# End of a chunked scan reordered: where the yT rows are converted, and where the projection begins

## The reference, cut to what matters

```python
# branch A, per chunk of 128 tokens (8 chunks for the prompt)
lmat   = exp(where(tril, diff, -inf))                       # decay masks, 16 heads
cb     = einsum('bclgn,bcsgn->bclsg', cm, bm)
y_diag = einsum('bclsg,bclsge,bcsgep->bclgep', cb, lmat, xdt)
final, prev = lax.scan(step, init_state, (chunk_decay, st)) # s = s * dec + add
y_off  = einsum('bclgn,bcgepn,bclge->bclgep', cm, prev, exp(acs))
y      = rmsnorm((y_diag + y_off + d_skip * xs) * silu(z), ssd_norm_w)
# merge
merged = g0 * (y_ssd @ w_br_ssd) + g1 * (y_att @ w_br_att) + g2 * (y_mem @ w_br_mem)
y      = rmsnorm(x + merged @ w_out, norm_f_w)
```

## Time and profile before

| | us |
|---|---|
| runs (3) | 2124.83, 2127.19, 2128.45; median 2127.19 |
| profiled execution | 2122.49, span 2120.6 |
| TensorE busy | 1978.7 (93% of the span) |
| VectorE, ScalarE, GpSimd busy | 984.6, 763.9, 241.5 |

### The profile page before, as it was taken

How to read it: one execution, slowest core, us unless ns; L and a number is a source line. 1 busy time by engine, 2 the same in 40 slices (tenths; PEclk the granted TensorE clock), 3 DMA queues, 4 the chain that set the end, 5 groups by cost and what they waited for, 6 DMA issues and landing times.

```text
span 2120.6 us, 34809 instructions
## 1 busy us (share of the span) xinstructions
PE 1978.7 (93%) x14301; PEld 1887.0 (89%) x14301; DVE 984.6 (46%) x1941; ACT 763.9 (36%) x1642; POOL 241.5 (11%) x358
## 2 busy tenths in 40 slices
PE   5999999999979999999999899999999859969997
PEld 5899999999979999999999898769999759969997
DVE  5313676535465353534236676103454545454423
ACT  5223354223343333323555322215566532132202
POOL 1001111100001010111111200001121111100000
PEclk9999999999999999999999999999999869989999
DMA  6211332311101111122246675683455536454422
GB/s 216 90 42 52 93 92 82 93 46 48 40 30 51 54 49 57 61 64 83 68 147 220 224 255 163 228 281 124 150 160 176 202 102 191 166 181 137 144 83 105
DMA packets 171742, 257.18 MB, mean 121 GB/s; under 512 B 20229, under 2 KB 115269, under 8 KB 171557
## 3 DMA queue, kind: packets, MB, share of 16 engines
q1 hardware_dynamic: 149328, 187.97, 28.1%
q0 software_dynamic: 22256, 66.98, 9.3%
HBM read 188.13 MB, written 66.76 MB: 120 GB/s over the span
## 4 chain that ended last, share of the span: by engine, by line
PE 76%; DVE 8%; ACT 6%; DMA 5%; issue 3%; SPq 0%; DVEq 0%; POOL 0%; ACTq 0%; POOLq 0%
PE bank L2287 19%; PE bank L2288 19%; PE bank L2289 19%; PE bank L2483 2%; DVE w_lo L1753 2%; PE bank L2698 2%; PE bank L2458 2%; DMA acc<-acc_T 2%; PE bank L2441 1%; PE bank L2587 1%; PE bank L2419 1%; ACT soft L1579 1%; PE bank L2742 1%; PE bank L2520 1%; DMA sums<-sum_T 1%
## 5 line engine op out<-in xcount | busy, mean ns | idle before, releaser
L2287 PE MATMUL bank<-w_hi,hT_hi 128*128 128x256 f32 (+1 forms) x1848 | 535.7, 290 | 1.4 <-issue 1.4
L2288 PE MATMUL bank<-w_lo,hT_hi 128*128 128x256 f32 (+1 forms) x1848 | 523.8, 283 | 0.0
L2289 PE MATMUL bank<-w_hi,hT_lo 128*128 128x256 f32 (+1 forms) x1848 | 522.9, 283 | 0.0
L2287 PE MATMUL bank<-hT_hi,w_hi 128*128 128x352 f32 x1344 | 450.8, 335 | 6.3 <-DVE acc L2134 5.6
L2289 PE MATMUL bank<-hT_hi,w_lo 128*128 128x352 f32 x1344 | 438.9, 327 | 0.0
L2288 PE MATMUL bank<-hT_lo,w_hi 128*128 128x352 f32 x1344 | 438.2, 326 | 0.0
L2287 PEld LDWEIGHTS bank<-w_hi,hT_hi 128*128 128x128 f32 (+1 forms) x1848 | 348.7, 189 | 3.2 <-issue 1.6
L2289 PEld LDWEIGHTS bank<-w_hi,hT_lo 128*128 128x128 f32 (+1 forms) x1848 | 349.6, 189 | 0.6
L2288 PEld LDWEIGHTS bank<-w_lo,hT_hi 128*128 128x128 f32 (+1 forms) x1848 | 348.7, 189 | 1.3
L2287 PEld LDWEIGHTS bank<-hT_hi,w_hi 128*128 128x128 f32 x1344 | 257.7, 192 | 20.1 <-issue 8.4
L2288 PEld LDWEIGHTS bank<-hT_lo,w_hi 128*128 128x128 f32 x1344 | 258.5, 192 | 0.5
(11 more groups left out here) (423 smaller groups left out, 2926.1 us busy)
## 6 DMA issues: line engine op xcount, KB each, us to landing
w_raw<-in_w_in SPq DMA_DIRECT2D x96, 512.0 KB, 5.0
kvring<-in_cache_win_kv SPq DMA_DIRECT2D x98, 256.0 KB, 4.7
feat_T<-fstage POOLq DMA_DIRECT2D x40, 528.0 KB, 4.0
fstage<-feat_T SPq DMA_DIRECT2D x16, 528.0 KB, 4.6
xc<-feat_T SPq DMA_DIRECT2D x8, 1024.0 KB, 5.8
sums<-sum_T SPq DMA_DIRECT2D x32, 256.0 KB, 4.5
o_rows<-obuf POOLq DMA_DIRECT2D x48, 132.0 KB, 2.0
mo<-o_rows SPq DMA_DIRECT2D x24, 264.0 KB, 3.6
```

The lines of the kernel that those rows point to most:

```text
L2287: pe.matmul(out, xh(k), wh(k), start=(k == 0), stop=False)
L2288: pe.matmul(out, xh(k), wl(k), start=False, stop=False)
L2289: ins = pe.matmul(out, xl(k), wh(k), start=False, stop=(k == nk - 1))
```

## The change

Up to the gates' last projection the list is the same. Behind it (ssd 6,1), (6,2), (5,6) and (6,3) come first, and the yT rows are loaded and converted behind them; four rows must be done for the first projection step, all eight for the fourth (before: eight for the first). The first three projection steps stand between, each alone. The two decay halves of chunk 7 are apart, the second between rows 5 and 6. The w_lo of the last gate chunk's successor comes behind (ssd 7,3). The slots of the rows follow `YA_SLOT`. The splits of chunks 52 to 55 are attached to their last step, and the remaining 45 steps are spread over 54 groups (before 52 steps and splits over 51 groups), with empty groups behind (7,5), (8,5), (8,6).

```diff
--- before.py
+++ after.py
@@ -113,6 +113,7 @@
 
 N_MEM_FILL, N_TAIL_FILL = 8, 2
 FILL_MERGE, FILL_KEYS, FILL_SOFT, FILL_VALUES = 3.75, 2.25, 1.25, 1.75
+YA_SLOT = (0, 1, 2, 0, 1, 0, 1, 0)
 PASSES = ((1, 4),)
 PASS_AT = {1: 0}
 
@@ -301,21 +302,13 @@
     for c in range(NB):
         core.append([("ssd", c, 0)] + ([("ssd", c - 1, 5)] if c else []))
         core += [[("ssd", c, 1 + i)] + [("decay", 0, i)] * (c == 0) for i in range(2)]
-        core.append(([("ssd", c - 1, 6)] if c else []) + [("ssd", c, 3)] + [("decay", c + 1, i) for i in range(2) if c + 1 < NB])
+        core.append(([("ssd", c - 1, 6)] if c else []) + [("ssd", c, 3)])
+        core[-1] += [("decay", c + 1, i) for i in range(2) if c + 1 < NB - 1]
         core.append([("ssd", c, 4)])
-    core += [[("ssd", NB - 1, 5)], [("ssd", NB - 1, 6)], [("ssd_state",)], [("ssd", NB, 0)]]
-    core += [[("ssd", NB, q)] for q in (1, 2, 3)]
-    core += [[(q, b)] for b in range(BS) for q in ("ssd_sb", "ssd_sd", "ssd_so")]
-    core += [[("ssd_st",)], [("ssd_sy",)]]
-    core += [[("ssd", NB, q)] for q in (4, 5, 6)] + [[], []] + [[("yb", k)] for k in range(KT8)]
-    n_gate, n_ya = 31, 4
+    n_gate = 5 * (NB - 2) + 1
     core[n_gate - 3] += [("yal", k) for k in range(3)]
-    for i in range(n_ya):
-        core[n_gate + i] += [("yal", k) for k in ((3, 4), (5, 6), (7,), ())[i]]
-        core[n_gate + i] += [("ya", 2 * i), ("ya", 2 * i + 1)]
     sched += spread(core[:n_gate], gate_steps(len(fill_src)))
-    for x in core[n_gate:n_gate + n_ya]:
-        sched += x
+    last_gate = len(chunks) - 1
     steps = []
     for i in range(4):
         n = chunk("p1", 2 * i, "att+mem", CW * i)
@@ -326,8 +319,19 @@
                     steps.append([("p1", n, f, br, j)])
                     if j == 0 and (ft, br) != (0, 0) and ft + br < KT8:
                         steps[-1].append(("p1g", ft + br, 1 - br))
-        steps.append([("split", n)])
-    sched += spread(core[n_gate + n_ya:], steps)
+        steps[-1].append(("split", n))
+    c = NB - 2
+    sched += [("ssd", c, 1), ("ssd", c, 2), ("ssd", c - 1, 6), ("ssd", c, 3)]
+    sched += [("yal", 3), ("ya", 0), ("yal", 4), ("ya", 1), ("ya", 2), ("yal", 5), ("ya", 3)] + steps[0]
+    sched += [("ssd", c, 4)] + steps[1] + [("decay", c + 1, 0), ("yal", 6), ("ssd", c + 1, 0), ("ssd", c, 5)] + steps[2]
+    sched += [("yal", 7), ("ya", 4), ("ya", 5), ("decay", c + 1, 1), ("ya", 6), ("ya", 7)]
+    core = [[("ssd", c + 1, 1)], [("ssd", c + 1, 2)], [("ssd", c, 6), ("ssd", c + 1, 3)], [("low", last_gate)], [("ssd", c + 1, 4)]]
+    core += [[("ssd", NB - 1, 5)], [], [("ssd", NB - 1, 6)], [("ssd_state",)], [("ssd", NB, 0)]]
+    core += [[("ssd", NB, q)] for q in (1, 2, 3)]
+    core += [[(q, b)] for b in range(BS) for q in ("ssd_sb", "ssd_sd", "ssd_so")]
+    core += [[("ssd_st",)], [("ssd_sy",)], [("ssd", NB, 4)], [("ssd", NB, 5)], [], [], [("ssd", NB, 6)], [], []]
+    core += [[("yb", k)] for k in range(KT8)]
+    sched += spread(core, steps[3:])
     for i in range(4):
         n = chunk("p2", 2 * i, "w_br_ssd", CW * i)
         sched += [("p2", n, f, j) for f in range(2) for j in range(3)] + [("split", n)]
@@ -966,7 +970,11 @@
             return (Lflat[:, D:2 * D] if b % 2 == 0 else yo[:, :]).rearrange("p (i n) -> p i n", i=8)
 
         def ya_slot(k):
-            return (yraw, acc1, acc0)[k % 3][:, :]
+            return (yraw, acc1, acc0)[YA_SLOT[k]][:, :]
+
+        def ya_loads(at, k):
+
+            return 16 * sum(YA_SLOT[x] == at for x in range(k))
 
         def acc_of(ft):
             return (acc0, acc1)[ft % 2]
@@ -1158,8 +1166,8 @@
                     if k == 0:
                         late_free(sp)
                     if k >= 3:
-                        sp.wait_ge(s_yal, k - 2)
-                    sp.dma_start(ya_slot(k), yT[8 + k]).then_inc(s_kv[k % 3], 16)
+                        sp.wait_ge(s_yal, 1 + max(x for x in range(k) if YA_SLOT[x] == YA_SLOT[k]))
+                    sp.dma_start(ya_slot(k), yT[8 + k]).then_inc(s_kv[YA_SLOT[k]], 16)
                     if k == 3:
                         gates_stored(sp)
                         load_gate(0, 0)
@@ -1655,12 +1663,12 @@
                     k = s[1]
                     if k == 0:
                         act.wait_ge(s_pj, n_act_proj)
-                    act.wait_ge(s_kv[k % 3], kv_loads(k % 3) + 16 * (k // 3 + 1))
+                    act.wait_ge(s_kv[YA_SLOT[k]], kv_loads(YA_SLOT[k]) + ya_loads(YA_SLOT[k], k + 1))
                     act.activation(yAh[:, k, :], ya_slot(k), ACT.Copy).then_inc(s_yah, 1)
                 elif s[0] == "yb":
                     k = s[1]
                     at = k % 3
-                    act.wait_ge(s_kv[at], kv_loads(at) + 16 * len(range(at, KT8, 3)) + 16 * (k // 3 + 1))
+                    act.wait_ge(s_kv[at], kv_loads(at) + ya_loads(at, KT8) + 16 * (k // 3 + 1))
                     if k == 6:
                         act.wait_ge(s_p1st[0], 16 * KT8 // 2)
                     act.activation(yBh[:, k, :], yb_slot(k), ACT.Copy).then_inc(s_yah, 1)
@@ -2130,7 +2138,7 @@
                         if ft >= 2 and j == 0:
                             dve.wait_ge(s_p1st[ft % 2], 16 * (ft // 2))
                         elif j == 0:
-                            dve.wait_ge(s_yal, KT8)
+                            dve.wait_ge(s_yal, 1 + max(x for x in range(KT8) if YA_SLOT[x] == 2 - ft))
                         dve.tensor_tensor(acc1[:, cols], psum, gate1[:, 0, cols], ALU.mult).then_inc(s_pjv, 1)
                     else:
                         dve.tensor_tensor(gate1[:, 1, cols], psum, gate1[:, 1, cols], ALU.mult).then_inc(s_pjv, 1)
@@ -2617,6 +2625,8 @@
                         started.add(n)
                         pe.wait_ge(s_wlo, n + 1)
                     if s[0] == "p1" and u == n_act_proj:
+                        pe.wait_ge(s_yal, KT8 // 2)
+                    if s[0] == "p1" and u == n_act_proj + 3:
                         pe.wait_ge(s_yal, KT8)
                     if s[0] == "p2" and s[2:] == (0, 0) and chunks[n][1] == 0:
                         pe.wait_ge(s_yal, KT8 + KT8)
```

## The result

The kernel after takes 2139.0 us, median of 5 runs (2133.99 to 2145.75), against 2125.56 before (5 runs, 2124.83 to 2128.45). The ratio is 1.0067, with a 95% interval of 1.0050 to 1.0084: slower, by 13.4 us. The profiled execution took 2141.32 us, 18.8 more than that of before (2122.49), so the traces show some 5 us more than the medians do. The forecast was 2132.4, +5.2.

The account below looks back on a forecast made before the run. It took latency chains through four queues, not busy times, as what the change acts on, with TensorE 93% busy. 3.2 + 5.6 - 3.6 = +5.2 us on the median of 2127.2 gave 2132.4, range 2116 to 2141.

Parts of the forecast that it names:

- Part A: Chunks 6 and 7, up to chunk 7's state: 3.2 us lost, bounds -5 to +8.
- The bound of 3.3 us for row 3: Row 3's load behind xc: 7.2 us expected to land, with bounds of 3.3 and 8.
- Rival 1: Before the fourth projection step: the eight-row wait of 12.7 us does not form, -10.4 us, 2116.8; chance of faster 0.25.
- Part B, the waits: The sample's masks: 4.2 us idle behind w_hi plus 1.4 at ssd_sb 0, together 5.6; bounds 0 to 9.
- Rival 2: Weights in time for the sample's masks: -0.4 us, 2126.8; chance 0.25, with smaller errors elsewhere.
- Part B, the fillers and the clock: The sample's 24 steps with 20 fillers instead of some 24: no cost, up to 3 us if a state load is late.
- 9, the clock falls too: Upper bound of the loss at the sample's masks: 9 us if the clock falls too, against 5.6 in the sum.
- The 3 us bound: The sample's steps with fewer fillers: up to 3 us lost if a state load is late.
- Part C: The last norm and the lower rows: -0.9 and -2.7, together 3.6 us won; bounds -8 to 0.
- 47 us behind L2753: Sign at the end: the last projection comes 47 us behind L2753 instead of 49.7.
- The clock as a loose end of 3 us: Five restarts may each cost 0 or 2 to 3 us; the sum moves some 3 us either way between builds.
- Rival 4: Row 3 and state loads late, half clock in all gaps: +8 + 9 + 0 = +17, 2144; chance 0.08.

Follow-up runs that it names:

- experiment 4: The kernel after with SyncE's load of row 3 put ahead of chunk 7's xc load: 2137.64 us, ratio 1.0056 against before.
- kernel 9: The kernel after with the splits of chunks 52 and 53 put back behind ssd_sb 0 and ssd_sd 4, no filler moved: 2132.91 us, 1.0034 against before.
- kernels 5 and 6: The kernel before with fillers moved: four more bare pairs of state update and output, 2132.98 us (1.0029); its one bare pair parted, 2120.98 us (0.9976).
- kernels 7: The kernel after with splits 52 and 53 put back and three fillers moved ahead of ssd_st, ssd_sy and ssd_sb 0: 2124.56 us, 0.9999 against before.
- kernel 3: The kernel after with only the split of chunk 52 put back behind ssd_sb 0: 2134.04 us, ratio 1.0045 against before.
- the front alone: The kernel after with splits as steps of their own and empty groups removed, new order of chunks 6 and 7 kept: 2136.87 us, 1.0056 against before.

## Why the prediction was right in direction and short in size

**The front, Part A: right.** Set 1.5 us back for the later start, the steps are: y from the state ends at 1690.1 (forecast 1688; at half clock, 3.65 us), first projection step 1699.8 (1698), increment 1707.4 (1705.8), all eight rows 1730.4 (1729), chunk 7's second increment 1750.9 (1750.9). The waits: 9.7 for row 3 (9 to 10), 14.4 for the eight rows (12.7), 5.7 for the state (5.8). The first slip of 2 us was still 1.4 at the eight rows, where the chain on ScalarE and not TensorE set the time, and went behind them: from there to the increment it took 20.5 us instead of 21.9. That the end agrees to 0.1 us is luck. The bound of 3.3 us for row 3 did not come true: it was taken 6.8 us after its issue and 7.2 after that of `xc`, as the neighbour row of 6.5 had said.

The Trainium skill (DMA: Bandwidth & Descriptors, Queues, rings and completion order) says that completion need not follow the order of issue, but also that a DMA's semaphore increment lands only after every earlier write of the same DMA engine. The prediction took the first half alone; by the second, no overtaking of `xc` was promised. The trace shows none: the row issued second was taken 6.8 us later. Of the 2.7 us that the wait lost when it was issued first (experiment 4), 2.6 are its earlier issue.

**Rival 1, the eight-row wait absent: fell.** It measured 14.4 us, and decides below 7.5. The reason given against it held: rows 4 and 5 stand behind a norm on ScalarE, rows 6 and 7 behind the masks. In the trace the former were taken at 1720.01 and row 6 at 1726.90; the late load of row 7 added 1.5.

**Part B, the waits: right.** 3.78 us before the sample's y (forecast 4.2), and 1.46 at `ssd_sb` 0 (1.4). ScalarE after shows the reason, the weight chunk between the two halves of the masks:

```profile
1776.45 1.91 ACT L1433 ACTIVATE w_hi<-w_raw 128x2048 fp32r<-128x2048 f32 x1 [1.65 <-DMA w_raw<-in_w_br_mem]
1778.26 0.77 ACT L1452 ACTIVATE Lm<-bank,sc 32x32 f32<-32x32 f32 x4
```

Rival 2, the weights in time, fell with it.

**Part B, the fillers and the clock: here it failed.** The term was "The sample's 24 steps have 20 fillers instead of some 24; at about two engines' slack I cost that at nothing, and up to 3 us if a state load is late". It measured 11.3 us in this trace: 12.8, less the 1.46 of `ssd_sb` 0. TensorE idled only 2 us more; the rest is clock. The 29 us at half clock lie in three spells (from stretches of 4 us):

| spell | what stands ahead of it | at half clock | cost |
|---|---|---|---|
| 1780 to 1792 | waits of 3.78 and 1.46 us | 10 | 5 |
| 1840 to 1856 | a wait of 1.96 us | 14 | 7 |
| 1872 to 1878 | no idle time; `ssd_so` 7 and `ssd_st` without a filler between | 5 | 2.5 |

Together 14.5 us; less the 3.6 that before's one spell cost (7.2 at half), this is the 10.9 above.

So two steps of the prediction were wrong. It priced the clock behind Part B's own waits in a bound only ("9, the clock falls too") and left it out of the sum: with the first spell Part B's waits come to some 10 us, not 5.6. And it weighed the fillers as cover for waits of others, and looked for a fallen clock behind gaps alone. They also keep the clock up where nothing waits. The row to ask was in the trace before, at 1816 to 1824 (PE busy 4.00, clock 0.62 and 0.53), behind a bare pair:

```profile
1816.00:1820.00 4.00, 4.00 (x22) 4.00 (x23) 2.51 (x9) 1.91 (x1) 1.18 (x2) 0.62 0.48 170
1820.00:1824.00 4.00, 4.00 (x18) 3.93 (x17) 2.44 (x2) 0.01 (x1) 0.00 (x0) 0.53 1.02 353
```

The 3 us bound had the wrong mechanism too. The one wait among the states behind `ssd_sb` 0 was no late state load but another low part in the way: split 53, attached, stood ahead of `ssd_sd` 4, and VectorE made `w_lo` first.

```profile
1835.42 2.29 DVE L1761 TENSOR_TENSOR w_lo<-w_raw,w_hi 128x2048 fp32r<-128x2048 f32 x1 [6.56 <-ACT w_hi L1433]
1837.63 0.47 DVE L2257 TENSOR_SCALAR xc<-btok,con 32x512 f32<-32x512 f32 x1
1838.03 2.14 DVE L2262 SCALAR_TENSOR_TENSOR Lm<-xc,sc,bank 128x128 f32<-128x128 f32 x8
```

Behind that wait of 1.96 us the granted clock after was

```profile
1840.00:1844.00 4.00, 3.69 (x20) 3.49 (x21) 3.15 (x10) 0.00 (x0) 0.90 (x1) 0.70 0.58 173
1844.00:1848.00 4.00, 4.00 (x18) 4.00 (x17) 2.13 (x7) 0.00 (x0) 0.89 (x1) 0.50 0.87 289
1848.00:1852.00 4.00, 4.00 (x19) 4.00 (x20) 0.00 (x0) 0.25 (x1) 0.00 (x0) 0.50 0.58 202
1852.00:1856.00 4.00, 4.00 (x19) 3.62 (x18) 0.69 (x2) 0.84 (x2) 0.00 (x0) 0.59 0.00 0
```

so that 2 us of idle time cost 7 more in clock: 0.30 + 0.50 + 0.50 + 0.41 of 4 us each. In kernel 9, with split 53 put back, wait and spell are gone. A place without a filler is the end of the states, where `ssd_so` 7 and `ssd_st` follow each other (timeline of TensorE after, and the clock behind them).

```profile
1869.81 1.85 PE L2331 MATMUL bank<-xc,state 128*128 128x4 f32 x16
1871.51 2.83 PE L2331 MATMUL bank<-xc,xdt 128*128 128x4 f32 x16
```

```profile
1872.00:1876.00 4.00, 4.00 (x19) 4.00 (x20) 0.00 (x0) 1.36 (x2) 0.00 (x0) 0.54 1.00 321
```

That the fillers' place is enough for such a loss, and for its absence, is shown by kernels 5 and 6. That three fillers are about half of the loss in the kernel after is shown by kernels 7 and 9; but the one ahead of `ssd_sb` 0 also takes 1.0 us of idle time away there, so the share of the bare places alone is not shown.

How long a spell lasts differs between executions of the same list. The first one is 3.4 us at half clock in kernel 3 and 9.4 in kernel 9, which are alike up to there; the second is 14 us in the kernel after and 3.4 in kernel 4, behind waits of 1.96 and 1.39. So the sizes in the table are those of one execution, and only the medians say what a place costs.

**Part C: right, smaller.** -2.3 against -3.6. From `ssd_sy` to the norm 14.91 us (forecast 14.35), with a wait of 5.5 as said; the rows won 1.9 instead of 2.7. "47 us behind L2753" had dropped the 1.05 us of the sum itself, which gives 48.1; it measured 49.4.

**The clock as a loose end of 3 us: too small.** It was priced for restarts behind gaps. In the profile, half clock in the states' stretch alone was 22 us more, 11 us of time. Rival 4 (2144) was right on the sample's side: its +9 stands for Part B's waits with a fallen clock, which measured some 10. Its +8 for the front was wrong, where half clock in fact fell from 46.5 to 33.9 and the loss was 3.3. That the profile came near its total is a coincidence.

The sum with the measured sizes is 3.3 + 3.8 + 12.8 - 2.3 = 17.6, and 1.5 - 0.2 for what lies around gives 18.9 between the profiles. The medians give 13.4. The runs of the kernel after spread over 12 us, those of before over 4 in that comparison (up to 11 in the later ones). Kernel 4's trace, 6.9 us shorter in the states with the same list there, points at the clock in that stretch; no kernel was profiled twice, so this is not shown.

The Trainium skill (TensorE: Matmul & The Clock Gate, Part 1) says that the default is throttled and activity releases the throttle. Kernels 5 and 6 fit it only if activity is something else than what the profile counts as busy: 4.00 of 4.00 us busy stood beside a clock of 0.50.

## What to carry to other kernels

Before steps that keep TensorE fed are moved, write down what then stands next to what: two groups of small matmuls that meet without a full one between can cost the clock for some microseconds, though the engine shows no idle time, and so can an idle time of 1 to 2 us among them. Price the clock behind every wait that is forecast. Look at the granted clock in stretches of 4 us beside the busy column, in the kernel as it is: one such dip shows what a second one can cost. And compare two orders by the segments between fixed marks, each step credited; the total of an experiment that moves fillers ("the front alone") names the wrong cause.

## What the runs showed of the hardware

- The granted clock fell to half while TensorE counted as fully busy, behind sixteen matmuls of 32x128 and sixteen of 128x4, some 4 us together: 27.8 us at half clock in the states' stretch with five such pairs, 0.0 with none, at 640 and 641 recorded matmuls. Two times sixteen of 128x4 were followed by 0.54 in the kernel after and by 1.00 in kernel 3.
- Behind idle times of 1.96 and 1.39 us among the sample's states, with the same list, the clock fell to 0.50 for 14 us of half clock in one execution (kernel after) and to 0.73 at the lowest, 3.4 us, in another (kernel 4).
- A 528 KB row issued 0.4 us behind the 1 MB load of `xc` was taken 6.8 us after its issue; issued 1.7 us ahead of `xc` (kernel 4) it took 6.1, and the row that was issued with two gate loads close behind it, and no `xc`, took 3.3.
- The part of the program whose list no kernel changed, up to chunk 6's first increment, ended between 1675.1 and 1681.7 us over the profiled executions looked at. So a difference of a few us between two traces has to be looked for by stretch before it is given to an edit.
